# Starting a token mixer with the first attention's values, one token tile at a time, and placing the indexer's dots between two later weight units

## The reference

```python
xn = rms_norm(x, norm_mix_g)                       # x: output of the first block's last layer norm
proj = xn @ w_in                                   # 1024 x 7752
qa, ka, va, qb, kb, vb, qi, ki, wi, xc, yc, gates = split(proj)
y_a = moba_attention(heads(qa), heads(ka), heads(va), rel_bias[:, :8])
# indexer of the second attention:
dots  = einsum('bqhd,bsd->bqhs', qi, ki)           # 8 index heads
score = einsum('bqh,bqhs->bqs', wi, relu(dots)) * idx_scale
idx   = top_k(score, 64)                           # only these keys are attended to
y_b = dsa_attention(heads(qb), heads(kb), heads(vb), idx, rel_bias[:, 8:])
y_c = rg_lru(conv(xc)) * gelu(yc)
x = x + (sum of gated y_a @ w_pa, y_b @ w_pb, y_c @ w_pc) @ w_o
x = x + relu(rms_norm(x) @ w_up)**2 @ w_down ; out = rms_norm(x)
```

## Time and profile before

| | |
|---|---|
| median of 3 runs | 978.35 us |
| the profiled execution's own time | 978.27 us |
| its span, first to last instruction | 976.5 us |
| TensorE busy | 961.0 us (98%) |
| VectorE busy | 675.0 us (69%) |
| ScalarE busy | 468.3 us (48%) |
| TensorE's granted clock, mean | 0.999 |

### The profile page before, as it was taken

The page is one execution under the profiler, slowest core; times in us unless marked ns, Lnnn a source line. Parts: engine busy times, 40 slices in busy tenths (PEclk is TensorE's granted clock), DMA queues, the critical chain, the costliest instruction groups (busy, mean ns, idle before and its releaser), DMA issues.

```text
span 976.5 us, 15425 instructions
## 1 busy us (share of the span) xinstructions
PE 961.0 (98%) x5927; PEld 848.3 (87%) x5927; DVE 675.0 (69%) x968; ACT 468.3 (48%) x721; POOL 35.0 (4%) x63
## 2 busy tenths in 40 slices
PE   9999999999999999999999999999999999999997
PEld 7888888888898888888888789999999888888886
DVE  3886767676787876767677577876876666666663
ACT  3543434345666454444335556566654454343432
POOL 2100001000000000000001000000000000000000
PEclk9999999999999999999999999999999999999999
DMA  8766676639533565656554655445565546565541
GB/s 292 238 215 202 202 225 209 205 136 252 167 124 100 180 208 196 223 183 203 183 152 163 189 157 130 130 130 157 168 196 187 199 131 215 174 202 184 195 150 43
DMA packets 142160, 175.67 MB, mean 180 GB/s; under 512 B 7152, under 2 KB 121009, under 8 KB 142110
## 3 DMA queue, kind: packets, MB, share of 16 engines
q1 hardware_dynamic: 138896, 166.55, 52.8%
q0 software_dynamic: 2656, 8.31, 2.6%
q10 hardware_dynamic: 558, 0.12, 0.1%
HBM read 173.88 MB, written 1.09 MB: 179 GB/s over the span
## 4 chain that ended last, share of the span: by engine, by line
PE 94%; DVE 2%; ACT 1%; issue 1%; POOL 0%; DVEq 0%; POOLq 0%
PE bank L501 93%; PE bank L757 1%; DVE x_both L1413 1%; DVE x_rows L1434 0%; DVE stats L1426 0%; DVE x_rows L1439 0%; ACT x_both L1055 0%; PE bank L634 0%; ACT arena L1278 0%; ACT arena L1176 0%; ACT arena L1302 0%; PE bank L646 0%; POOL rstd L1910 0%; DVE vareps L1403 0%; ACT arena L1207 0%
## 5 line engine op out<-in xcount | busy, mean ns | idle before, releaser
L501 PE MATMUL bank<-x_both,w_hi 128*128 128x256 f32 (+1 forms) x2112 | 436.3, 330 | 1.9 <-ACT arena L1207 1.1
L1028 DVE TENSOR_TENSOR w_lo<-raw,w_hi 128x1024 fp32r<-128x1024 f32 x308 | 362.7, 1221 | 95.1 <-ACT w_hi L1016 94.7
L501 PEld LDWEIGHTS bank<-x_both,w_hi 128*128 128x128 f32 x2112 | 355.8, 190 | 42.9 <-issue 6.6
L1016 ACT ACTIVATE w_hi<-raw 128x1024 fp32r<-128x1024 f32 x308 | 307.9, 1049 | 98.0 <-PE bank L501 93.5
L501 PE MATMUL bank<-x_both,w_lo 128*128 128x256 f32 (+1 forms) x1512 | 285.1, 283 | 0.0
L501 PEld LDWEIGHTS bank<-x_both,w_lo 128*128 128x128 f32 (+1 forms) x1512 | 229.1, 191 | 3.0
L501 PE MATMUL bank<-w_hi,arena_r 128*128 128x512 f32 x672 | 190.8, 392 | 0.2 <-DVE arena_r L1560 0.2
L501 PEld LDWEIGHTS bank<-w_hi,arena_r 128*128 128x128 f32 x672 | 124.8, 188 | 26.5 <-issue 0.8
L501 PE MATMUL bank<-w_lo,arena_r 128*128 128x512 f32 x336 | 106.6, 391 | 0.0
L1483 DVE TENSOR_REDUCE arena<-bank 128x512 f32<-128x1024 f32 x57 | 69.7, 1222 | 48.6 <-PE bank L501 48.6
L501 PEld LDWEIGHTS bank<-w_lo,arena_r 128*128 128x128 f32 x336 | 63.1, 188 | 13.8
(11 more groups left out here) (168 smaller groups left out, 603.8 us busy)
## 6 DMA issues: line engine op xcount, KB each, us to landing
raw<-w_up SPq DMA_DIRECT2D x76, 512.0 KB, 4.5
raw<-w_down SPq DMA_DIRECT2D x76, 512.0 KB, 4.2
raw<-w_in SPq DMA_DIRECT2D x60, 512.0 KB, 4.6
raw<-w_gate SPq DMA_DIRECT2D x44, 512.0 KB, 4.7
raw<-w_qkv SPq DMA_DIRECT2D x24, 512.0 KB, 4.8
raw<-w_o SPq DMA_DIRECT2D x16, 512.0 KB, 4.1
table<-bias_vectors POOLq DMA_DIRECT2D x12, 256.0 KB, 4.2
raw<-w_pa SPq DMA_DIRECT2D x4, 512.0 KB, 4.2
```

The lines of the kernel that those rows point to most:

```text
L501: return nc.tensor.matmul(*a, skip_group_check=True, **k)
L1016: nc.scalar.activation(w_hi[slot][:, c], raw[slot][:, c], ACT.Copy).then_inc(hi_done, 1)
L1028: last = nc.vector.tensor_tensor(w_lo[slot][:, c], raw[slot][:, c], w_hi[slot][:, c].bitcast(F32), ALU.subtract)
```

## The change

The units VA and VA+1 become the first of the mixer, ahead of QI; their loads, too. TensorE computes them with a function of its own, `pe_first_values`: products of tile 0 start when tile 0's quarters of `x_both` are there, and tile 1's transposes come behind them. `with_gain` and the second norm of tile 0 are done before tile 1's statistics, tile 0's `v_low` between the two passes over tile 1. Of the fillers 6, 5 and 4 are left. The dots of four pairs of index heads now all lie in VB and VB+1, one behind each tile of 12 matmuls. TensorE's wait for the copied values and the last relus moves from behind VB+1 to ahead of the first score of the MOBA attention.

```diff
-U_QI = U_FFN[1] + 3 * NCH
+U_VA = U_FFN[1] + 3 * NCH
+U_QI = U_VA + 2
 U_KI = U_QI + 2
-U_VA = U_KI + 1
-U_VB = U_VA + 2
+U_VB = U_KI + 1
...
             for j in range(2):
+                load_unit(eng, U_VA + j, by_rows(w, 4 * j, 4, O_VA, 512))
+            for j in range(2):
                 load_unit(eng, U_QI + j, by_rows(w, 0, KT, O_QI + 256 * j, 256))
             load_unit(eng, U_KI, by_rows(w, 0, KT, O_KI, 72))
-            for j in range(2):
-                load_unit(eng, U_VA + j, by_rows(w, 4 * j, 4, O_VA, 512))
...
@@ def pe_score
+            if a == A_MOBA:
+                eng.wait_ge(v_copied, 3)
+                eng.wait_ge(dots_relu, 8)
...
+        def pe_first_values(eng):
+
+            va = [[bank[0][:, :]], [bank[1][:, :]]]
+            whi, wlo = (part(w, (U_VA + 1) % SLOTS, 4) for w in (w_hi, w_lo))
+
+            def second(i, w, sources, stop):
+                for k in range(4):
+                    for src in sources:
+                        last = mm(va[i][0], src[:, 4 + k, i * P:(i + 1) * P], w[:, k, :], start=False,
+                                  stop=(stop and k == 3))
+                return last
+
+            keep_warm(bank[5], 6)
+            pe_norm(eng, 4, nbuf, ((0, 0), (0, 1)))
+            keep_warm(bank[5], 5)
+            eng.wait_ge(lo_done, U_VA + 1)
+            eng.wait_ge(x_ready, 4 * 4 + 1)
+            rows(U_VA % SLOTS, va, x_hi, x_lo, 0, 4, 512, True, False, (0,))
+            eng.wait_ge(hi_done, 2 * (U_VA + 1) + 2)
+            eng.wait_ge(x_ready, 4 * 4 + 2)
+            second(0, whi, (x_hi, x_lo), False)
+            pe_norm(eng, 4, nbuf, ((1, 0), (1, 1)))
+            keep_warm(bank[4], 4)
+            eng.wait_ge(x_ready, 4 * 4 + 3)
+            rows(U_VA % SLOTS, va, x_hi, x_lo, 0, 4, 512, True, False, (1,)).then_inc(unit_done, 1)
+            eng.wait_ge(x_ready, 4 * 4 + 4)
+            second(1, whi, (x_hi, x_lo), False)
+            eng.wait_ge(lo_done, U_VA + 2)
+            second(0, wlo, (x_hi,), True)
+            second(1, wlo, (x_hi,), True).then_inc(unit_done, 1)
...
@@ def pe_mixer
-                elif U_VA <= unit < U_MOBA:
-                    j = (unit - U_VA) % 2
-                    if unit == U_VB:
+                elif U_VB <= unit < U_MOBA:
+                    j = unit - U_VB
+                    if j == 0:
                         eng.wait_ge(v_copied, 2)
-                    last = rows(s, [[bank[0][:, :]], [bank[1][:, :]]], x_hi, x_lo, 4 * j, 4, 512, j == 0, j == 1)
-                elif unit == U_QI:
-                    last = first_project(eng, unit, 4)
+                    for i in range(NT):
+                        last = rows(s, [[bank[0][:, :]], [bank[1][:, :]]], x_hi, x_lo, 4 * j, 4, 512, j == 0, j == 1,
+                                    (i,))
+                        if i == 1:
+                            last.then_inc(unit_done, 1)
+                        if (i, j) == (0, 0):
...
+                        pe_dots(eng, 2 * j + i)
...
-                if unit == U_VB + 1:
-                    eng.wait_ge(v_copied, 3)
-                    eng.wait_ge(dots_relu, 8)
...
@@ block.tensor
-            keep_warm(bank[5], 12)
-            pe_norm_end(eng, 4, nbuf, 12, 4)
+            pe_first_values(eng)
...
@@ s_mixer
+                if U_VB <= unit < U_MOBA:
+                    s_dots(eng, 2 * (unit - U_VB))
                 if unit in (U_VA + 1, U_VB + 1):
...
-                if U_VA <= unit < U_MOBA:
-                    s_dots(eng, unit - U_VA)
+                if U_VB <= unit < U_MOBA:
+                    s_dots(eng, 2 * (unit - U_VB) + 1)
...
@@ block.scalar
             s_rms(eng, 0, (0,))
             scaled(0)
+            s_rounds(eng, 4, (0,))
+            s_split(eng, U_VA + 1)
             s_rms(eng, 0, (1,))
-            s_rounds(eng, 4, (0,))
             scaled(1)
             s_rounds(eng, 4, (1,))
-            s_split(eng, U_QI + 1)
             s_mixer(eng)
```

More of the change, by code:

```diff
@@ L106, in mixer_turns @@
     started, scored, applied = A_MOBA, A_MOBA, A_MOBA
-    for unit in range(U_QI, U_GATE):
+    for unit in range(U_VA, U_GATE):
         apply = applied if applied < scored else None
@@ L545, in first_apart @@
             return apart(banks, wlo, SEQ, range(KT), False)
[L547 to L558, removed]
         def row_phase(eng, unit, rounds, begin):
@@ L800, in pe_dots @@
             last.then_inc(dotted, 1)
+        def pe_first_values(eng):
[25 more added lines that the diff above has]
+            second(1, wlo, (x_hi,), True).then_inc(unit_done, 1)
         def pe_mixer(eng):
             score_unit = {step_of(u): u for u in range(U_QI, U_GATE)}
-            for unit, apply, score_step in TURNS:
+            for unit, apply, score_step in TURNS[2:]:
                 if apply is not None:
@@ L817, in pe_mixer @@
                                      x_lo[:, k, :], k == 0, k == KT - 1)
-                elif U_VA <= unit < U_MOBA:
-                    j = (unit - U_VA) % 2
-                    if unit == U_VB:
+                elif U_VB <= unit < U_MOBA:
+                    j = unit - U_VB
+                    if j == 0:
                         eng.wait_ge(v_copied, 2)
-                    last = rows(s, [[bank[0][:, :]], [bank[1][:, :]]], x_hi, x_lo, 4 * j, 4, 512, j == 0, j == 1)
-                elif unit == U_QI:
-                    last = first_project(eng, unit, 4)
+                    for i in range(NT):
[4 more added lines that the diff above has]
+                        if (i, j) == (0, 0):
+                            eng.wait_ge(proj_copied, COPIED[U_KI] + 1)
+                            for n in range(NT):
+                                last = nc.tensor.transpose(bank[5][:, IDX_HEADS * n:IDX_HEADS * (n + 1)],
+                                                           wi_t[:, n * P:(n + 1) * P], ident[DH:KI_COLS, DH:KI_COLS])
+                            last.then_inc(wi_turned, 1)
+                        pe_dots(eng, 2 * j + i)
                 else:
                     last = project(s, proj_out(unit), x_hi, x_lo)
-                last.then_inc(unit_done, 1)
-                if U_VA <= unit < U_MOBA:
[L829 to L835, removed]
-                if unit == U_VB + 1:
-                    eng.wait_ge(v_copied, 3)
-                    eng.wait_ge(dots_relu, 8)
+                if not U_VB <= unit < U_MOBA:
+                    last.then_inc(unit_done, 1)
                 if apply is not None:
@@ L1356, in scaled @@
             def scaled(i):
-                eng.wait_ge(rstd_ready, 13 + i)
+                eng.wait_ge(rstd_ready, 12 + 2 * i)
                 for h in range(2):
@@ L1429, in v_statistics, with v_rows @@
             return variance(slice(i, i + 1), mv[:, i, 1:2], 1.0, LN_EPS)
-        def v_rows(eng, link, i, n, ready):
+        def v_rows(eng, link, i, n, ready, between=None):
             for h in range(2):
@@ L1436, in v_rows @@
             link(last)
+            if between:
+                between()
             eng.wait_ge(rstd_ready, n)
@@ L1681, in v_mixer @@
                     v_probs(eng, link, score_step)
-                if U_VA <= unit < U_MOBA:
-                    v_dots(eng, link, unit - U_VA)
+                if U_VB <= unit < U_MOBA:
+                    for g in range(2):
+                        v_dots(eng, link, 2 * (unit - U_VB) + g)
                 if U_MOBA - 1 <= unit < U_MOBA - 1 + TOPK // 8:
@@ L1857, in _, with tile0_low @@
             with_gain(0, 0)
-            n = v_statistics(eng, link, 1, ffn_done)
-            rms_variance(eng, link, 0, 0)
             eng.wait_ge(z_ready, 2)
             with_gain(0, 1)
-            v_rows(eng, link, 1, n, z_ready)
-            eng.wait_ge(z_ready, 3)
-            with_gain(1, 0)
+            rms_variance(eng, link, 0, 0)
+            n = v_statistics(eng, link, 1, ffn_done)
+            def tile0_low():
+                v_low(eng, 4, 0, 0)
+                v_low(eng, 4, 0, 1)
+            v_rows(eng, link, 1, n, z_ready, tile0_low)
+            for h in range(2):
+                eng.wait_ge(z_ready, 3 + h)
+                with_gain(1, h)
             rms_variance(eng, link, 0, 1)
[L1866 to L1869, removed]
             v_low(eng, 4, 1, 0)
             v_low(eng, 4, 1, 1)
-            v_split(eng, U_QI + 1)
+            v_split(eng, U_VA + 1)
             v_mixer(eng, link)
@@ L1970, in _ @@
                 toeplitz(2 * j, 16 + 2 * j).then_inc(table2_in, 16)
-            ln_roots()
-            ln_roots()
+            for i in range(NT):
+                done[1] = i
+                ln_root()
+                ln_root()
             eng.wait_ge(n_ready, 20)
```

3 lines of the change are left out of this document (1 added, 2 removed).

## The result

| | before | after |
|---|---|---|
| median | 978.35 us (977.91 to 978.86, 5 runs) | 972.56 us (972.39 to 973.03, 5 runs) |
| profiled execution, its own time | 978.27 us | 972.43 us |
| its span | 976.5 us | 970.6 us |
| TensorE busy | 961.0 us (98%) | 958.1 us (99%) |
| granted clock, mean | 0.999 | 0.998 |

The ratio after to before is 0.9936, with an interval of 0.9925 to 0.9946: faster by 0.6%. The two medians alone give 972.56 / 978.35 = 0.9941. The change was measured twice more, and gave 0.9946 (0.9934 to 0.9958) and 0.9937 (0.9925 to 0.9949).

A forecast was written before the change was run, and what follows sets the result against it. TensorE, busy 98% of the span, was taken as the bound; only its waits could be won. 3.75 (part 1) + 1.66 (waits) = 5.41, less 0.1: 978.27 - 5.3 = 973.0 us, range 972.2 to 975.4.

The forecast's parts named there:

- Tile 0: In the transition, 20 products of tile 0 (VA, VA+1) start at 520.3 and fill 4.55 us of TensorE's wait.
- What tile 1 pays: In the transition, tile 1's scaling, and with it its first product, comes 0.8 us later; 1.2 with a slow root.
- Part 1: Products of tile 0 inside the transition: 4.55 us less tile 1's 0.8 us delay, 3.75 us won.
- The root: GpSimd's root for tile 1's second norm takes 0.55 us instead of 0.92, as no gain runs beside it.
- The two waits: TensorE's waits behind the dots before VB (0.47 us) and behind VB+1 (1.19 us) both go: 1.66 us won.
- The deduction of 0.1: 0.1 us taken off the summed gain for changes of form where a tile's row is cut.
- Dots between tiles: In VB and VB+1, waits of closer-spaced dots for relus cost nothing; one that fails costs at most 1.19 us.
- The first probabilities: VectorE's first probabilities, behind VB+1, have 1.0 us of slack and are at worst 0.2 us late.
- part 1's upper bound: In the transition, 4.5 us won if TensorE never waited for tile 1; 6.1 us won in all, giving 972.2.
- Rival (c): TensorE's clock falls to half rate in the transition, doubling the 10.9 us of VA and VA+1: 983.9 us; chance 0.04.

The follow-up runs named there:

- the experiment beside a gain: Changed kernel with tile 1's second-norm variance moved between its two gains, so GpSimd's root runs beside a gain: 973.31 us, ratio 0.9945.
- beside a low part: Changed kernel with VA+1's low part made ahead of tile 1's low parts and tile 0's four products with it replacing the last 4 fillers: 972.99 us, ratio 0.9941.

## Why the prediction came out as it did

Direction, mechanism and the median agree: 973.0 was forecast and 972.56 found, inside the range. By the ratio to the runs beside it, though, the time is 978.35 x 0.9936 = 972.1 us, 0.1 under the range's low end of 972.2. By the steps:

- **Tile 0.** Products were to start at 520.3, on the scale of the trace of before, where the net's last product is at 516.38; on that scale they started at 520.26. The 20 products take their 4.6 us. Held back, they cost 4.62. Right.
- **What tile 1 pays.** This is the term of the sum that was mis-sized: 0.8 us, and 0.55 measured. Scaling was to be 0.8 us later and is 0.65 (523.94 - 516.16 against 523.51 - 516.38), and the way from scaling to product is 2.84 us, not the 2.94 that I carried over. The links ahead of scaling were each a little shorter than taken: the second pass starts 4.25 us behind the net's last product (taken: 4.37), the variance 6.78 (taken: 6.97). Part 1 gives 5.57 - 1.66 = 3.9 instead of 3.75.
- **The root** takes 0.55 us, as taken. The trace showed it in part only; the experiment beside a gain (0.93) and beside a low part (1.46) settle it. By the rule of the Trainium skill (GPSIMD Engine Reference, § 1. Specifications), that GpSimd contends with VectorE instructions of two SBUF inputs, this was to be so. These runs agree, but for the root that had begun ahead of its gain (0.55 us).
- **The two waits.** 1.66 us were forecast. The second alone is 1.2 us, taken out of the kernel before or put back into the changed one. Of the first, 0.47, I made no kernel; that the product behind dots now comes after 0.87 us there is in the trace.
- **The deduction of 0.1** for changes of form was right in size: 4.55 - 0.55 + 1.66 = 5.66, and 5.57 us are measured. The work behind tile 1's start, without the waits, is 52.34 - 10.07 - 1.66 = 40.61 us before and 46.77 - 10.62 = 36.15 now, so moving the 20 products saves 4.46 us, not 4.55.
- **Dots between tiles** cost nothing: 0.86 or 0.87 us at all four. The first probabilities end at 575.7 and are needed at 576.35, 0.6 us of slack left of 1.0, where I allowed for their being 0.2 us late.
- **The step that failed** is thus tile 1's payment of 0.8 us in part 1. With the measured 0.55 in its place the sum is 5.56, and the changed stretch gives 5.57. That alone does not bring the time out of the range, as 978.35 - 5.57 is 972.8. The other 0.7 us down to 972.1 are not in the changed stretch.
- **The range** left no room for them. Its low end was made from part 1's upper bound alone, while one execution's start-up differs from another's by tenths, and by more than 2 us in two of the profiles here. The interval of the ratio reaches from 971.0 to 973.1 us, and the two repeats give 973.1 and 972.2 on the same scale: on which side of 972.2 a single measurement falls is chance.
- **Rival (c)** was judged right for this kernel and for a partly wrong reason. I wrote that 1.3 us of holes had cost no clock before. True, but these were split by fillers (0.56, 0.56 and 0.22 us); without fillers holes of 1.34 and 1.12 us cost 1.5 us. Its price was too high: the level lasted about 3.5 us, not for all of the 48 products.

Not tried: the loads in their old order, and fewer than four dots in VB and VB+1.

## What to carry to other kernels

Where a row of matmuls waits for the last of several tiles, put first a product that can be cut by tiles, and judge the wait by the chain of the last tile: 4.55 us of work moved into the hole cost 0.55 us of delay to that chain. Ask what the other engines do beside a short GpSimd operation on the path; a two-input subtraction beside it nearly tripled it here. And when a hole gets shorter, count the fillers anew: too many stand in front of the first tile, too few cost the clock. Fillers also hide in a trace which engine ends a wait; take the last ones out once to see it.

## What the runs showed of the hardware that I had not expected

- GpSimd's root of 128 x 1 numbers took 0.55 us alone, 0.93 beside a 0.68 us multiplication of two SBUF tensors, and 1.46 beside two 1.2 us subtractions of SBUF tensors; once the subtraction was moved behind it, it took 0.55 again. It also took 0.55 with such a multiplication beside it that began 0.09 us after the root.
- Without fillers the granted clock fell about 0.4 us after products had begun again, not in the holes: 0.98 at 520 to 521, 0.50 from 521 to 524. With one hole of 1 us behind 4.6 us of products it stayed at 1.00.
- The changed stretch of 34.5 us repeated within 0.01 us in three profiles, while the program's first 14 us took up to 2.6 us longer. In both profiles that started late the granted clock stood at 0.50 for 2 to 3 us there, between 10 and 13 us.
